# Stacking high and low halves of queries and keys for the differential scores of heads 2 to 7

## What is computed

```python
proj = h @ w_in[l]                       # q, k, v, u: 512 columns each
q, k = ...reshape(S, 8 heads, 2, 32)     # two score maps per head
s = (q . k) * 32 ** -0.5 - slope[h] * |qpos - kpos|
p = softmax(s)
a = p[:, :, 0] - lam * p[:, :, 1]        # the differential map of a head
o = rms(a @ v) * subln_g * (1 - lam_init)
f = real(fft over time and columns of u) @ w_f + b_f
h = layer_norm(alpha * h + concat(o, f) @ w_o)
h = layer_norm(alpha * h + swiglu(h))
```

## Time and profile before

| | before |
|---|---|
| median of 3 runs | 918.43 us |
| the profiled execution, time | 918.89 us |
| its span | 917.1 us |
| PE busy | 900.9 us (98%) |
| DVE busy | 594.3 us (65%) |
| ACT busy | 486.8 us (53%) |
| POOL busy | 116.4 us (13%) |

### The profile page before, as it was taken

How to read it: one execution, slowest core, us unless ns; L and a number is a source line. 1 busy time by engine, 2 the same in 40 slices (tenths; PEclk the granted TensorE clock), 3 DMA queues, 4 the chain that set the end, 5 groups by cost and what they waited for, 6 DMA issues and landing times.

```text
span 917.1 us, 13492 instructions
## 1 busy us (share of the span) xinstructions
PE 900.9 (98%) x4942; PEld 762.5 (83%) x4942; DVE 594.3 (65%) x1082; ACT 486.8 (53%) x795; POOL 116.4 (13%) x110
## 2 busy tenths in 40 slices
PE   9999999999999999999999999999999999999996
PEld 7999878889888879887888888888978788888885
DVE  4898677686768685867655445556685964545454
ACT  4955757567686464764543434325674454334431
POOL 4643864102000010002000000000001100000000
PEclk9999999999999999999999999999999999999999
DMA  9655232573534137332565555544332365555521
GB/s 350 237 194 171 91 123 89 199 259 139 187 128 145 59 112 301 109 122 92 195 238 197 170 212 194 170 152 177 147 138 93 141 225 184 183 187 181 196 80 46
DMA packets 22379, 151.59 MB, mean 165 GB/s; under 512 B 2608, under 2 KB 3120, under 8 KB 4528
## 3 DMA queue, kind: packets, MB, share of 16 engines
q1 hardware_dynamic: 20304, 142.62, 43.4%
q10 hardware_dynamic: 2016, 8.16, 2.4%
HBM read 149.72 MB, written 1.05 MB: 164 GB/s over the span
## 4 chain that ended last, share of the span: by engine, by line
PE 57%; DVE 3%; ACT 2%; issue 1%; POOL 0%; DVEq 0%; POOLq 0%; ACTq 0%
PE ps L516 12%; PE ps L522 12%; PE ps L518 12%; PE ps L1166 5%; PE ps L819 2%; PE ps L821 2%; PE ps L820 2%; PE ps L1184 2%; PE ps L565 1%; PE ps L1228 1%; PE ps L1108 1%; PE ps L549 1%; PE ps L547 1%; PE ps L545 1%; PE ps L861 1%; DVE wlo L1846 1%
## 5 line engine op out<-in xcount | busy, mean ns | idle before, releaser
L1352 ACT CAST whi<-raw 128x2048 fp32r<-128x2048 f32 (+1 forms) x127 | 241.6, 1906 | 141.4 <-PE ps L522 112.5
L1846 DVE TENSOR_TENSOR wlo<-raw,whi 128x1024 fp32r<-128x1024 f32 x127 | 162.3, 1278 | 137.8 <-ACT whi L1352 137.4
L516 PE MATMUL ps<-whi,ahi 128*128 128x512 f32 (+2 forms) x432 | 166.7, 386 | 0.1
L518 PE MATMUL ps<-wlo,ahi 128*128 128x512 f32 (+2 forms) x432 | 165.8, 384 | 0.0
L522 PE MATMUL ps<-whi,alo 128*128 128x512 f32 (+2 forms) x432 | 164.8, 384 | 0.0
L1852 DVE TENSOR_TENSOR wlo<-raw,whi 128x1024 fp32r<-128x1024 f32 x107 | 130.5, 1220 | 0.0
L516 PEld LDWEIGHTS ps<-whi,ahi 128*128 128x128 f32 x432 | 81.1, 188 | 16.9 <-issue 0.9
L522 PEld LDWEIGHTS ps<-whi,alo 128*128 128x128 f32 x432 | 81.1, 188 | 15.8
L518 PEld LDWEIGHTS ps<-wlo,ahi 128*128 128x128 f32 x432 | 81.2, 188 | 15.4
L516 PE MATMUL ps<-whi,bhi 128*128 128x512 f32 x174 | 69.8, 401 | 0.4 <-issue 0.3
L545 PE MATMUL ps<-ahi,whi 128*128 128x256 f32 x240 | 68.4, 285 | 0.0
(11 more groups left out here) (300 smaller groups left out, 1743.6 us busy)
## 6 DMA issues: line engine op xcount, KB each, us to landing
raw<-in_wstream SPq DMA_DIRECT2D x133, 1024.0 KB, 4.8
par<-in_params ACTq DMA_DIRECT2D x5, 1024.0 KB, 4.8
tab<-in_tables ACTq DMA_DIRECT2D x1, 1370.0 KB, 10.0
res<-in_x SPq DMA_DIRECT2D x2, 512.0 KB, 4.6
raw<-in_wstream SPq DMA_DIRECT2D x2, 512.0 KB, 6.4
out<-res SPq DMA_DIRECT2D x4, 256.0 KB, 2.0
par<-in_params ACTq DMA_DIRECT2D x1, 512.0 KB, 4.2
arena<-in_wf ACTq DMA_DIRECT2D x2, 256.0 KB, 5.1
```

Source lines behind the costliest of these rows:

```text
L516: pe.matmul(banks[b][:, 0:cw], h_, wh[:, i, c], start=st, stop=False, skip_group_check=True)
L518: pe.matmul(banks[b][:, 0:cw], h_, wl[:, i, c], start=False, stop=False, skip_group_check=True)
L1352: act.copy(whi[:, u % SPL, c], raw[:, u % RAW, c]).then_inc(w_hi, 1)
L1846: dve.tensor_tensor(wlo[:, u % SPL, c], raw[:, u % RAW, c], whi[:, u % SPL, c].bitcast(F32), ALU.subtract).then_inc(w_lo_v, 1)
```

## The change

1. **Heads 2 to 7 in one pass.** The columns of the `qk` weight units are sorted by map, so that each piece of q or k holds four heads, 32 partitions each. ACT writes its high half (`qk_hi`), DVE its low half (the new `qk_lo`, `qk_done`). For each of heads 2 to 7, GpSimd's DMA queue copies three blocks of 32 partitions into one of three buffers (`stack_head`): q high with k high, q low with k high, q high with k low. A float32r product of depth 96 then gives the sum of the three products. The buffers are `wst` (widened), `bhi` and `blo`; from head 5 on a buffer is used again, and the copies wait until the scores of the head three before are done. The scores of a head still are four products of 128x256.
2. **Heads 0 and 1 stay in float32.** ACT writes another copy of 64 partitions for them (`qkf`, `qk_wide`).
3. **Waits.** The products of one map now wait for that map's minimum of the head before, not for both.
4. **Places.** Eight side pieces instead of three stand ahead of the scores of head 0. The table of pieces by the end of steps -2 to 7 was 0, 12, 22, 32, 36, 40, 44, 48, 48, 48 and is 0, 13, 23, 33, 40, 45, 48, 48, 48, 48. In step 3 all pieces stand ahead of the scores of head 4, so that 45 of 48 are done there, where it was 38. ACT's `qk_out(3)` moves up between the exponentials of the two maps of head 2.

```diff
 def side_pieces(h):
-    return (0, 12, 22, 32, 36, 40, 44)[h + 2] if h < 5 else 48
+    return (0, 13, 23, 33, 40, 45)[h + 2] if h < 4 else 48
+FIRST_SCORES = 8
+WIDE = 2
+STACKED = ((0, 0), (1, 0), (0, 1))
+RING = 3
...
                 def diff_scores(h):
                     if h == 0:
-                        pe.wait_ge(qk_done, 4 * l + 2)
                         pe.wait_ge(cw_done, 3 * l + 3)
...
-                    if h >= 1:
-                        pe.wait_ge(ds_max, 2 * NH * l + 2 * h)
-                    for t in range(T):
-                        for c in range(2):
...
-                            mm = pe.matmul(X[c][:, t * S:(t + 1) * S],
-                                           qkt[rr, n // 4, t * P:(t + 1) * P], qkt[rr, 4 + n // 4, :],
+                        pe.wait_ge(qk_wide, 2 * l + 2)
+                    if h < WIDE:
+                        q_, k_ = (qkf[h * HD:(h + 1) * HD, s, :, :] for s in range(2))
+                    else:
+                        pe.wait_ge(stacked[h % RING], stack_uses(l, h))
+                        rows_ = slice(0, HD * len(STACKED))
+                        q_, k_ = (stack[h % RING][rows_, s, :, :] for s in range(2))
+                    for c in range(2):
+                        if h >= 1:
+                            pe.wait_ge(ds_max, 2 * NH * l + 2 * h - 1 + c)
+                        for t in range(T):
+                            mm = pe.matmul(X[c][:, t * S:(t + 1) * S], q_[:, c, t * P:(t + 1) * P], k_[:, c, :],
...
-                for n in range(3):
+                for n in range(FIRST_SCORES):
                     side_piece(n)
                 diff_scores(0)
...
-                    mid = (n0 + n1) // 2
+                    mid = n1 if h == NH // 2 - 1 else (n0 + n1) // 2
...
+                def qk_lo(i):
+                    j = QK_ORDER.index(i)
+                    dve.wait_ge(qk_hi, 4 * l + j + 1)
...
+            def stack_head(l, h):
+                if h == WIDE:
+                    pool.wait_ge(qk_done, 4 * l + 2)
+                if h == NH // 2:
+                    pool.wait_ge(qk_done, 4 * l + 4)
+                if h >= WIDE + RING:
+                    pool.wait_ge(ds_psum, 2 * NH * l + 2 * (h - RING) + 2)
+                m, at_ = h % 4, qks_at[h // 4]
+                for b, (fq, fk) in enumerate(STACKED):
+                    first, step_ = 512 * fq, 1024 + 512 * (fk - fq)
+                    src = arena[m * HD:(m + 1) * HD, at_ + first:at_ + first + 2 * step_]
+                    pool.dma_start(stack[h % RING][b * HD:(b + 1) * HD, :, :, :].rearrange("p s c t -> p s (c t)"),
+                                   src.rearrange("p (s x) -> p s x", s=2)[:, :, 0:512]
+                                   ).then_inc(stacked[h % RING], 16)
             for l in range(DEPTH):
+                for h in range(WIDE, NH):
+                    stack_head(l, h)
```

More of the change, by code:

```diff
@@ L268, in conv_src, with qk_part @@
             return G[b][:, n % 2 * S:(n % 2 + 1) * S]
+        def qk_part(i, low):
+            at_ = qks_at[i % 2] + (2 * (i // 2) + low) * 512
+            return arena[:, at_:at_ + 512]
         def acc_bank(n, t, b):
@@ L347, in build @@
         rtmp = arena[:, 12800:13312]
-        qkt = arena[:, 0:2048].rearrange("p (k c) -> p k c", k=8)
+        qks_at = (0, 10240)
+        qkf = arena[0:WIDE * HD, 3072:4096].rearrange("p (s c t) -> p s c t", s=2, c=2)
+        stack = [s_.rearrange("p k c -> p (k c)").rearrange("p (s c t) -> p s c t", s=2, c=2)
+                 for s_ in (bhi[:, 0:4, :], blo[:, 0:4, :], wst[:, :, :])]
         v2 = arena[:, 2048:3072].rearrange("p (t c) -> p t c", t=T)
@@ L407, in build @@
         r_final = sem("r_final")
-        qk_done, v_done, u_done = (sem("qk_done"), sem("v_done"), sem("u_done"))
+        qk_wide, qk_hi, qk_done, v_done, u_done = sem("qk_wide"), sem("qk_hi"), sem("qk_done"), sem("v_done"), sem("u_done")
+        stacked = [sem(f"stacked{r}") for r in range(RING)]
         ds_psum, ds_max, dp_done, da_done = sem("ds_psum"), sem("ds_max"), sem("dp_done"), sem("da_done")
@@ L571, in narrow @@
                 for k in range(KT):
-                    pe.matmul(out, wst[:, k, :], ah[:, k, :], start=(k == 0), stop=False,
+                    pe.matmul(out, wst[:, k, 0:64], ah[:, k, :], start=(k == 0), stop=False,
                               skip_group_check=True)
@@ L1232, in diff_pv @@
                     mm.then_inc(do_psum, 1)
-                for n in range(3):
+                for n in range(FIRST_SCORES):
                     side_piece(n)
                 diff_scores(0)
-                for n in range(3, side_pieces(-1)):
+                for n in range(FIRST_SCORES, side_pieces(-1)):
                     side_piece(n)
@@ L1719, in qk_out @@
                     bank = G[QK_ORDER.index(i) % 2]
+                    dst = qk_part(i, 0).bitcast(F32R)
+                    if i % 2 == 0:
+                        wide = qkf[:, i // 2, :, :].rearrange("p c t -> p (c t)")
+                        src = bank[0:WIDE * HD, :]
+                        if i == 0:
+                            ins = act.activation(wide, src, ACT.Identity, scale=const("q_scale")[0:WIDE * HD, 0:1])
+                        else:
+                            ins = act.copy(wide, src)
+                        ins.then_inc(qk_wide, 1)
                     if i < 2:
-                        for j in range(2):
-                            ins = act.activation(qkt[:, 2 * i + j, :], bank[:, j * S:(j + 1) * S], ACT.Identity,
-                                                 scale=const("q_scale")[:, 2 * i + j:2 * i + j + 1])
-                    else:
-                        ins = act.copy(qkt[:, 2 * i:2 * i + 2, :], bank.rearrange("p (k c) -> p k c", k=2))
-                    ins.then_inc(qk_done, 1)
+                        ins = act.activation(dst, bank, ACT.Identity, scale=const("q_scale")[:, i:i + 1])
+                    else:
+                        ins = act.copy(dst, bank)
+                    ins.then_inc(qk_hi, 1)
                 split.until(("qk", l, 0))
@@ L2394, in _ @@
                 dve.tensor_copy(v2[:, 1, :], G[3]).then_inc(v_done, 1)
-                for i in QK_ORDER[:2]:
-                    split.until(("qk", l, i))
+                def qk_lo(i):
+                    j = QK_ORDER.index(i)
+                    dve.wait_ge(qk_hi, 4 * l + j + 1)
+                    bank, hi, lo = G[j % 2], qk_part(i, 0), qk_part(i, 1).bitcast(F32R)
+                    if i < 2:
+                        ins = dve.scalar_tensor_tensor(lo, bank, const("q_scale")[:, i:i + 1], hi, ALU.mult,
+                                                       ALU.subtract)
+                    else:
+                        ins = dve.tensor_tensor(lo, bank, hi, ALU.subtract)
+                    ins.then_inc(qk_done, 1)
+                split.until(("qk", l, 0))
+                qk_lo(0)
+                split.until(("qk", l, 2))
+                qk_lo(2)
                 def scores_max(n):
@@ L2441, in _ @@
                         scores_max(2 * h + 3)
+                    if h == 1:
+                        qk_lo(3)
                     if h < NH:
                         combine(h)
+                    if h == 0:
+                        qk_lo(1)
                     if h - 1 in D_SPLITS:
```

23 lines of the change are left out of this document (11 added, 12 removed).

## The result

The changed kernel takes **925.66 us** (median of 4 runs, 925.38 to 926.21), the kernel before 918.43 us beside it: a ratio of 1.0078, with a 95% interval from 1.0066 to 1.0091. The forecast was 918.8 us, the range 917.6 to 923.0: it is slower, and outside the range. The profiled execution took 925.67 us with a span of 923.9 us.

The account below looks back on a forecast made before the run. PE was taken as the bound, with the softmax on ACT and DVE about to be: Fourier products +0.91 us, old waits -0.74 us, so +0.17 us a layer, +0.34 us on 918.43 us: 918.8 us, range 917.6 to 923.

Parts of the forecast that it names:

- Heads 0 and 1 stay as they are: Float32 scores of heads 0 and 1 on PE: no change in their time, so no term in the sum.
- The clock falls in the idle time: Rival: granted clock drops while PE idles; 3 us of products at 1.2 GHz add 3 us a layer, 925 us; chance 0.04.
- The walk: Layer 0 from head 4's scores (384.30 us) through DVE and ACT to the Fourier products: 397.68 us, +0.91 us.
- The old waits: PE's waits at head 7's transposes (0.52 us) and a Fourier low half (0.22 us) fall away: -0.74 us a layer.
- The saving: Scores of heads 2 to 7 on PE: 0.76 us a head, 4.6 us a layer, 9.1 us in all.
- no rate gained: Rival: a stacked float32r product takes a float32 product's time; +1.7 us a layer, 921.8 us; chance 0.05.
- Late copies: Rival: GpSimd's copies delay heads 5 or 7 if an issue exceeds 1.73 us; 925.2 us at 2.0 us; chance 0.25.
- The signs I had named: Right: PE idles some 3 us before Fourier products, busy 9 us less. Wrong: buffer DMA waits, slow issues, clock under 1.

Follow-up runs that it names:

- the run with row blocks: The changed kernel with the two maps of heads 0 and 1 put back on different blocks of 32 partitions: 921.99 us, ratio 1.0039.
- Filled idle time: The changed kernel with 20 products of 128x512 that nobody reads added in PE's idle time of each layer: 921.57 us, ratio 1.0034.
- the last version: The changed kernel with only heads 2 and 3 stacked, others float32 with maps on different 32-partition blocks, side pieces at their old places: 915.50 us, ratio 0.9966.

## Why the prediction was wrong

**"Heads 0 and 1 stay as they are": the step that failed first.** I had priced their extra copy on ACT and not their products. The diff puts both maps of a head on the same 32 partitions (`qkf[h * HD:(h + 1) * HD]`), where the earlier trace rows show 8 products on 32 rows each in 1.13 us. I read that row as a price of the scores wherever they lie. The starts of its single products, in pairs 7 ns apart, were in the same trace and would have shown two streams side by side. The term that was missing is 0.86 us a head, 3.4 us in all; the run with row blocks measured 3.7 us.

**"The clock falls in the idle time", 0.04, was the other cause, and mis-sized twice.** I wrote that nothing like the idle time at the end of the span was forecast, while the forecast itself had PE idle for about 5 us a layer. As to the price, I took 3 us of products a layer; measured are 4.1 us for both layers. Filled idle time (921.57 us) shows it. No row stood behind the 3 us. That the rival's 925 us is near the result is chance: the sum is 3.7 and 4.1 us, less 0.6 us of overlap.

**The walk was right.** Scores of head 4 forecast at 384.30 us, measured at 385.43 us: 1.13 us late. The 1.72 us of heads 0 and 1 less the 0.37 us of the earlier entry would make 1.35 us, so the rest of the walk to there was priced 0.2 us too long. From there every step keeps this distance. DVE's low pass ends near 390.8 us (forecast 389.62 us), ACT's exponentials start at 391.65 us (390.50 us), its copy of u ends at

```profile
397.88 1.04 ACT L1805 COPY arena<-ps 128x512 f32<-128x512 f32 x2
398.82 0.58 ACT L1787 COPY arena<-ps 128x512 f32<-128x512 f32 x1
```

398.82 us (397.68 us). With the two missing terms taken out, the kernel took 918.47 us where the walk said 918.8 us. The old waits went as forecast; the way behind the Fourier products became 1.0 us a layer shorter by it, where I had 0.74 us.

**The saving** of 0.76 us a head was there (0.64 us rows in place of 1.13 us; the scores of head 5 and the product behind them start 0.48 us apart, at 387.94 and 388.42 us; 1.56 us for two heads in the last version), and the rival "no rate gained" falls. That it is lost to the places is confirmed, and more strongly than I had it: the places alone, with nothing saved, cost 7.8 us, the fallen clock's share included.

**Late copies**, given 0.25, are not the cause. An issue takes 0.51 us (three in 1.54 us, the row below), far under the 1.73 us that I worked out. No hold by DVE shows in them, though DVE was busy for 14.61 of the 18 us from 372 to 390 us; the one pause between two issues that nothing in the profile explains is 1.30 us, in layer 1. But I had sized them wrongly in two ways, and neither shows in the time only because ACT's copy of u comes later still. GpSimd's timeline and the page's DMA rows (KB each, median us to landing):

```profile
376.18 1.54 POOL L2687 DMA_DIRECT2D blo<-arena  x3 [12.53 <-DVE arena L2431]
377.71 1.55 POOL L2687 DMA_DIRECT2D wst<-arena  x3
379.24 1.61 POOL L2687 DMA_DIRECT2D bhi<-arena  x3
386.38 1.54 POOL L2687 DMA_DIRECT2D blo<-arena  x3 [5.53 <-PE ps L1206]
```

```profile
bhi<-arena POOLq DMA_DIRECT2D x12, 128.0 KB, 6.4
blo<-arena POOLq DMA_DIRECT2D x12, 128.0 KB, 4.4
```

The copies of heads 4 to 7 don't follow one another, as I had it: those of head 7 stand until the scores of head 4 have left their buffer, at 386.38 us. And a copy lands after 4.4 to 6.4 us, not 2.0 us. The Trainium skill (DMA: Bandwidth & Descriptors, Anatomy of one DMA) would have 2.3 us, an estimate by its formula for one DMA. The fastest of the 36 copies landed after 2.3 us, the median one after 5.2 us, the slowest after 11.0 us; so the trace agrees with the page at its least only, and the measured median decides.

**The signs I had named.** Of those for a wrong forecast, a granted clock under 1 in the stage is what the page shows, and waits of PE for copies into `bhi` and `blo` came too (1.5 and 1.2 us, in layer 1), though they cost nothing. Of those for a right one, the wait for ACT's copy ahead of the Fourier products came (2.24 and 1.23 us, where I had some 3 us) and the old waits went; PE was not 9 us less busy.

## What to carry to other kernels

When operands move to other partitions, read from the old rows which products run side by side, and price every block that shares a path with the edit, also one whose text says that it stays. A forecast that makes the busiest engine wait must price the work behind the wait at the lower clock, or say what fills the wait. And a saving is worth most on the path to the wait that ends last: two heads stacked ahead of it gave 3.0 us; six heads with later places lost 3.5 us, even with heads 0 and 1 on blocks of their own (921.99 against 918.52 us).

## What the chip showed that I had not expected

- Two streams of float32 products on different blocks of 32 partitions run side by side: 1.13 us for 8 products, 1.14 us when the loop goes map by map, and 1.99 us for 8 products on one block.
- The clock fell without a long wait. In layer 0 it was already falling in the stretch 394 to 396 us, when the longest single wait had been 0.76 us and PE had been busy for 1.54 and 1.12 us of two stretches of 2 us; it came back near 405 us, after PE had been busy without a pause since 398.97 us.
- A copy from SBUF to SBUF of 128 KB on GpSimd's queue is issued in 0.51 us and lands after 4.4 to 6.4 us at the median. Where it is the bound, the kernel's time spreads by 3.7 us over ten runs (915.76 to 919.48 us); in the change, where it is not, by 0.8 us over four. That the copies make this spread was not tried.
